# The last layer without the norm, turn and store of rows that no next layer reads; one row store per tile instead of two

## What is computed

```
h = RMSNorm(x) * norm_pre_mix[l]
z = h @ w_in[l]
mixer = concat(retention, mLSTM, gated DeltaNet, NSA)(z) @ w_out[l]
x = x + RMSNorm(mixer) * norm_post_mix[l]
x = x + RMSNorm(ConvFFN(RMSNorm(x) * norm_pre_ffn[l])) * norm_post_ffn[l]
```

## Time and profile before

| what | value |
|---|---|
| median of 3 runs | 4205.48 us |
| profiled execution, its own time | 4212.83 us |
| its span | 4211.0 us |
| TensorE busy | 3765.2 us (89%) |
| VectorE busy | 1950.8 us (46%) |
| ScalarE busy | 1286.9 us (31%) |
| DMA moved | 504.85 MB, mean 120 GB/s |
| mean granted TensorE clock | 0.946 of 2.4 GHz |

### The profile page before, as it was taken

The page is one execution under the profiler, slowest core; times in us unless marked ns, Lnnn a source line. Parts: engine busy times, 40 slices in busy tenths (PEclk is TensorE's granted clock), DMA queues, the critical chain, the costliest instruction groups (busy, mean ns, idle before and its releaser), DMA issues. The chain is left out here.

```text
span 4211.0 us, 55742 instructions
## 1 busy us (share of the span) xinstructions
PE 3765.2 (89%) x22236; PEld 3203.9 (76%) x22236; DVE 1950.8 (46%) x3830; ACT 1286.9 (31%) x2902; POOL 418.9 (10%) x296
## 2 busy tenths in 40 slices
PE   5999698688979999999979987977898899999997
PEld 4888587445658999997768876864475789999875
DVE  3234477663444333335541436776533443333455
ACT  2111255452222221123331114554432322211343
POOL 0035101002201000000000540010021100000000
PEclk9999799798989999999989998997899999999999
DMA  7344322305432222255543433122152422222654
GB/s 246 118 142 161 99 64 61 104 6 204 170 104 89 76 70 66 76 180 206 212 160 105 166 114 97 60 70 79 40 232 105 157 66 76 67 69 84 221 195 179
DMA packets 302046, 504.85 MB, mean 120 GB/s; under 512 B 67381, under 2 KB 226774, under 8 KB 297201
## 3 DMA queue, kind: packets, MB, share of 16 engines
q1 hardware_dynamic: 296523, 426.06, 31.3%
q0 software_dynamic: 4608, 67.11, 3.9%
q10 hardware_dynamic: 656, 8.13, 0.6%
HBM read 386.90 MB, written 129.63 MB: 123 GB/s over the span
## 5 line engine op out<-in xcount | busy, mean ns | idle before, releaser
L1033 PE MATMUL ps<-h_hi,fu_hi 128*128 128x344 f32 x2112 | 682.3, 323 | 10.1 <-DVE h_lo L1255 7.3
L1035 PE MATMUL ps<-h_hi,fu_lo 128*128 128x344 f32 x2112 | 677.6, 321 | 0.0
L1034 PE MATMUL ps<-h_lo,fu_hi 128*128 128x344 f32 x2112 | 677.1, 321 | 0.0
L564 PE MATMUL ps<-zi_whi,h_hi 128*128 128x468 f32 (+1 forms) x1152 | 432.9, 376 | 50.7 <-DVE zi_wlo L645 50.7
L1033 PEld LDWEIGHTS ps<-h_hi,fu_hi 128*128 128x128 f32 x2112 | 398.0, 188 | 14.1 <-DVE h_lo L1255 7.8
L1035 PEld LDWEIGHTS ps<-h_hi,fu_lo 128*128 128x128 f32 x2112 | 398.8, 189 | 0.0
L1034 PEld LDWEIGHTS ps<-h_lo,fu_hi 128*128 128x128 f32 x2112 | 398.2, 189 | 0.0
L568 PE MATMUL ps<-zi_wlo,h_hi 128*128 128x468 f32 (+1 forms) x1024 | 384.2, 375 | 0.0
L569 PE MATMUL ps<-zi_whi,h_lo 128*128 128x468 f32 (+1 forms) x1024 | 384.0, 375 | 0.0
L1059 PE MATMUL ps<-fd_whi,fd_fhi 128*128 128x512 f32 x704 | 278.4, 395 | 15.0 <-DVE fd_flo L1272 14.2
L564 PEld LDWEIGHTS ps<-zi_whi,h_hi 128*128 128x128 f32 x1152 | 217.5, 189 | 80.3 <-DVE h_lo L641 51.9
(11 more groups left out here) (633 smaller groups left out, 6964.2 us busy)
## 6 DMA issues: line engine op xcount, KB each, us to landing
w_ahead<-w_ffn_down SPq DMA_DIRECT2D x44, 1024.0 KB, 5.8
z<-zi_z SPq DMA_DIRECT2D x112, 234.0 KB
zi_h<-z SPq DMA_DIRECT2D x64, 384.0 KB, 4.6
f_all<-fu_f SPq DMA_DIRECT2D x44, 516.0 KB, 3.4
w_ahead<-w_ffn_gate SPq DMA_DIRECT2D x44, 512.0 KB, 4.8
w_ahead<-w_ffn_up SPq DMA_DIRECT2D x44, 512.0 KB, 6.1
fd_raw<-w_ffn_down SPq DMA_DIRECT2D x22, 1024.0 KB, 5.6
zi_raw<-w_in SPq DMA_DIRECT2D x24, 936.0 KB, 5.6
```

Source lines behind the costliest of these rows:

```text
L564: nc.tensor.matmul(out, rows_hi, w_hi[:, i % 2, k, c0], start=(k == 0), stop=False)
L1033: nc.tensor.matmul(out, up_hi[f % 2][:, j, k, :], h_hi[:, k, seg], start=(k == 0), stop=False)
L1034: nc.tensor.matmul(out, up_hi[f % 2][:, j, k, :], h_lo[:, k, seg], start=False, stop=False)
L1035: m = nc.tensor.matmul(out, up_lo[f % 2][:, j, k, :], h_hi[:, k, seg], start=False, stop=(k == KD - 1))
```

## The change

`FINAL` is true in the last layer. There the kernel now leaves out the whole chain from `norm_square` to `norm_store` for all nine tiles, and the load of the next norm's gain. `store(t)` now makes one DMA per tile in both layers: to the output in the last layer, to `x_cur` in the first. The counts that SyncE waits for at the end follow.

```diff
--- before.py
+++ after.py
@@ -712,6 +712,7 @@
     RING = 3
     STEPS = len(GROUPS) * NF
     MOST = max(e - a for a, e in GROUPS)
+    FINAL = l == DEPTH - 1
     STORE_AT = 5
     NORM_AT = {6: 0, 9: 1, 12: 2, 15: 3}
     H_STORE_AT = {7: 0, 8: 1, 9: 2, 10: 3}
@@ -813,6 +814,10 @@
 
             return GROUPS[g - 1][0] + f if g and f < GROUPS[g - 1][1] - GROUPS[g - 1][0] else None
 
+        def normed_tile(g, f, at):
+
+            return earlier(g, at[f]) if f in at and not FINAL else None
+
         def height(t):
             return min(P, TOK - t * P)
 
@@ -923,9 +928,9 @@
 
                 def store(t):
                     sp.wait_ge(S("x2_ready"), t + 1)
-                    sp.dma_start(x_cur[rows(t, height(t)), :], xt[0:height(t), t]).then_inc(S("x_stored"), 16)
+                    kept_row = x_cur[rows(t, height(t)), :]
                     out = io["y_prompt"][0, rows(t), :] if t < NT else io["y_sample"][:, 0, :]
-                    sp.dma_start(out, xt[0:height(t), t]).then_inc(S("x_stored"), 16)
+                    sp.dma_start(out if FINAL else kept_row, xt[0:height(t), t]).then_inc(S("x_stored"), 16)
 
                 other = Loads(sp, S("others"))
                 for pp in range(RING, len(GROUPS) * PAIRS):
@@ -938,21 +943,24 @@
                         sp.wait_ge(S("summed"), 6 * NF)
                         other(gb[:], io["norm_post_ffn"][ds(l, 1), :].rearrange("a n -> (a n)").partition_broadcast(P))
                         other(xt[:], x_cur[0:ROWS, :].rearrange("(t p) n -> p t n", p=P))
-                        norm_gain(kit, io, N, sp, 1 - l)
+                        if not FINAL:
+                            norm_gain(kit, io, N, sp, l + 1)
                     if g and p == STORE_AT:
                         for t in range(*GROUPS[g - 1]):
                             store(t)
-                    if p in H_STORE_AT and earlier(g, H_STORE_AT[p]) is not None:
-                        norm_store(kit, env, N, sp, earlier(g, H_STORE_AT[p]))
+                    if normed_tile(g, p, H_STORE_AT) is not None:
+                        norm_store(kit, env, N, sp, normed_tile(g, p, H_STORE_AT))
                 for t in range(*GROUPS[LAST]):
                     store(t)
-                    norm_store(kit, env, N, sp, t)
+                    if not FINAL:
+                        norm_store(kit, env, N, sp, t)
                 st.all_in()
                 ld.all_in()
                 for r in range(4):
                     sp.wait_ge(S(f"f_stored{r}"), 16 * ((NF - r + 3) // 4))
-                sp.wait_ge(S("x_stored"), 32 * TT)
-                norm_stored(kit, sp)
+                sp.wait_ge(S("x_stored"), 16 * TT)
+                if not FINAL:
+                    norm_stored(kit, sp)
                 other.all_in()
 
             @b.tensor
@@ -1062,9 +1070,9 @@
                         if f == NF - 1 and t + 1 < GROUPS[g_][1]:
                             m.then_inc(S("y_summed"), 1)
                     m.then_inc(S("used"), 1)
-                    if f in NORM_AT and earlier(g_, NORM_AT[f]) is not None:
-                        norm_turn(kit, env, N, pe, earlier(g_, NORM_AT[f]))
-                for t in range(*GROUPS[LAST]):
+                    if normed_tile(g_, f, NORM_AT) is not None:
+                        norm_turn(kit, env, N, pe, normed_tile(g_, f, NORM_AT))
+                for t in range(*GROUPS[LAST]) if not FINAL else ():
                     norm_turn(kit, env, N, pe, t, TAIL_BANK[t])
 
             @b.scalar
@@ -1178,20 +1186,22 @@
                     if s % NF == 0 and s:
                         for t in range(*GROUPS[s // NF - 1]):
                             square(t)
-                    if s % NF + 2 in NORM_AT and earlier(s // NF, NORM_AT[s % NF + 2]) is not None:
-                        norm_square(kit, N, act, earlier(s // NF, NORM_AT[s % NF + 2]))
+                    if normed_tile(s // NF, s % NF + 2, NORM_AT) is not None:
+                        norm_square(kit, N, act, normed_tile(s // NF, s % NF + 2, NORM_AT))
                 t = GROUPS[LAST][0]
                 square(t)
                 square(t + 1)
                 act.wait_ge(S("used"), NF * (LAST + 1))
                 A.activation(low_y[:], ps[LOW:LOW + NB, BANK:BANK + 2, :].rearrange("p a n -> p (a n)"), ACT.Copy).then_inc(S("low_read"), 1)
-                norm_square(kit, N, act, t)
-                norm_square(kit, N, act, t + 1)
+                if not FINAL:
+                    norm_square(kit, N, act, t)
+                    norm_square(kit, N, act, t + 1)
                 square(t + 2)
-                norm_scale_act(kit, N, act, t)
-                norm_scale_act(kit, N, act, t + 1)
-                norm_square(kit, N, act, t + 2)
-                norm_scale_act(kit, N, act, t + 2)
+                if not FINAL:
+                    norm_scale_act(kit, N, act, t)
+                    norm_scale_act(kit, N, act, t + 1)
+                    norm_square(kit, N, act, t + 2)
+                    norm_scale_act(kit, N, act, t + 2)
 
             @b.gpsimd
             def _(pool):
@@ -1202,12 +1212,12 @@
                 for g, (a, e) in enumerate(GROUPS):
                     for t in range(a, e):
                         n = height(t)
-                        if g == LAST and t == SAMPLE:
+                        if g == LAST and t == SAMPLE and not FINAL:
                             norm_root(kit, env, N, pool, t - 2)
                             norm_root(kit, env, N, pool, t - 1)
                         pool.wait_ge(S("y_eps"), t + 1)
                         nc.gpsimd.tensor_tensor(ss[0:n, 2, t:t + 1], ss[0:n, 1, t:t + 1], mhalf[0:n, 0:1], ALU.pow).then_inc(S("y_rms"), 1)
-                    for t in range(a, e) if g < LAST else (TT - 1,):
+                    for t in () if FINAL else range(a, e) if g < LAST else (TT - 1,):
                         norm_root(kit, env, N, pool, t)
 
             @b.vector
@@ -1274,7 +1284,7 @@
 
                 def take(t):
                     wait_sums(dve, t)
-                    if t >= N.depth:
+                    if t >= N.depth and not FINAL:
                         dve.wait_ge(S("x_turned"), t - N.depth + 1)
                     V.tensor_copy(N.row(t)[0:height(t)], sums(t)).then_inc(S("y_taken"), 1)
 
@@ -1287,7 +1297,8 @@
                         dve.wait_ge(S("y_taken"), t + 1)
                     else:
                         wait_sums(dve, t)
-                        dve.wait_ge(S("x_turned"), t - N.depth + 1)
+                        if not FINAL:
+                            dve.wait_ge(S("x_turned"), t - N.depth + 1)
                     dve.wait_ge(S("y_rms"), t + 1)
                     summed = low_y[:] if t == SAMPLE else row if group_of[t] < LAST else sums(t)
                     link(V.scalar_tensor_tensor(row, summed, ss[0:n, 2, t:t + 1], gb[0:n], ALU.mult, ALU.mult))
@@ -1355,24 +1366,26 @@
                     g_, f = s // NF, s % NF
                     if f >= 2 and earlier(g_, f - 2) is not None:
                         residual(earlier(g_, f - 2))
-                    if f + 1 in NORM_AT and earlier(g_, NORM_AT[f + 1]) is not None:
-                        norm_eps(kit, N, dve, earlier(g_, NORM_AT[f + 1]))
-                    if f in NORM_AT and earlier(g_, NORM_AT[f]) is not None:
-                        norm_scale(kit, N, dve, earlier(g_, NORM_AT[f]))
-                    if f - 1 in NORM_AT and earlier(g_, NORM_AT[f - 1]) is not None:
-                        norm_whole(kit, env, N, dve, earlier(g_, NORM_AT[f - 1]))
+                    if normed_tile(g_, f + 1, NORM_AT) is not None:
+                        norm_eps(kit, N, dve, normed_tile(g_, f + 1, NORM_AT))
+                    if normed_tile(g_, f, NORM_AT) is not None:
+                        norm_scale(kit, N, dve, normed_tile(g_, f, NORM_AT))
+                    if normed_tile(g_, f - 1, NORM_AT) is not None:
+                        norm_whole(kit, env, N, dve, normed_tile(g_, f - 1, NORM_AT))
                 t = GROUPS[LAST][0]
                 residual(t)
                 residual(t + 1)
-                norm_eps(kit, N, dve, t)
-                norm_eps(kit, N, dve, t + 1)
+                if not FINAL:
+                    norm_eps(kit, N, dve, t)
+                    norm_eps(kit, N, dve, t + 1)
                 dve.wait_ge(S("low_read"), 1)
                 link(V.tensor_tensor(low_y[:], ps[0:NB, BANK:BANK + 2, :].rearrange("p a n -> p (a n)"), low_y[:], ALU.add), S("sample_whole"))
                 residual(t + 2)
-                norm_whole(kit, env, N, dve, t, TAIL_BANK[t])
-                norm_eps(kit, N, dve, t + 2)
-                norm_whole(kit, env, N, dve, t + 1, TAIL_BANK[t + 1])
-                norm_whole(kit, env, N, dve, t + 2, TAIL_BANK[t + 2])
+                if not FINAL:
+                    norm_whole(kit, env, N, dve, t, TAIL_BANK[t])
+                    norm_eps(kit, N, dve, t + 2)
```

(2 more changed lines are left out.)

## The result

The changed kernel takes 4192.03 us (median of 9 runs, 4190.45 to 4208.24), the kernel before in the same series 4209.35 us (4198.74 to 4220.31). The ratio is 0.9965 with a 95% interval of 0.9954 to 0.9975: 0.35% less, or 14.7 us (10.5 to 19.4) of 4209.35, where 16.4 us were forecast. The interval leaves 1 out, so the changed kernel is faster, by less than 0.5%.

What follows compares the result with a forecast made beforehand. TensorE, busy 3765.2 of 4211.0 us, was taken as the bound, and at stage ends the chain there. Terms 5.2 + 10.0 + 1.2 = 16.4 us off the 4205.48 us median gave 4189.1 us; range 4178 to 4202 us, 8 in 10.

Steps and rivals of the forecast that it cites:

- Six turns: Second layer, tiles 0 to 5, inside the groups: eight transposes each, 0.87 us per turn, 5.2 us saved.
- squares, scalings and gains inside the groups: ScalarE and VectorE work removed in the second layer's groups: worth nothing, since TensorE's full stretches cover it.
- The second layer's tail: From the sample sum to the span's end: earlier sum, norm chain gone, sooner last landing; 10.0 us saved (9.3 to 10.5).
- The sample sum: VectorE in the second layer's tail: can start at 4191.44 in place of 4192.80, 1.36 us earlier.
- The unhindered small store: 32 KB store of the sample rows at the kernel's end: lands in 1.9 us, with 1.4 and 2.6 as ends.
- The first layer's end: Last h store lands in 2.6 us, not 4.0, so the second layer's first load comes earlier: 1.2 us (0 to 1.4).
- Stores inside the groups: Missing 512 KB stores in both layers' groups free DMA engines, but TensorE waits for no load there: 0 us.
- turns not given back: Rival: TensorE finds its inputs late inside the groups, so only 11.2 us are saved, 4194.3 us; chance 0.07.
- turns at full duration: Rival: the six turns cost 48 x 0.272 = 13.1 us, so 24.3 us are saved, 4181.2 us; chance 0.03.
- The granted clock: Rival: second layer's clock level shifts; around 4180 us (chance 0.14), 4200 us (0.07) or 4230 us (0.04).

Runs made afterwards that it cites:

- the doubled turns: Kernel before, with the eight transposes of each turn inside the groups issued twice, in both layers: ratio 1.0033 (1.0022 to 1.0045).
- the stores alone: Kernel before with one store per tile, whole norm chain kept in both layers: profiled once, no ratio; 21.5 us from tile 6's store to the end.
- the norm chain alone: Kernel before without the last layer's norm chain, both row stores kept in both layers: 4198.38 us against 4211.08, ratio 0.9969.
- the first stores put back: Changed kernel with the first layer's output stores put back: profiled once, no ratio; first layer's end 5.83 us, tail 12.75 us.
- the sum first: Changed kernel with the sample rows' sum ahead of tile 7's residual in the last layer's tail: ratio to before 0.9955 (0.9941 to 0.997).

## Why the prediction was right, point by point

- Six turns, forecast 5.2 us from 0.87 each: 5.5 us measured (2.74 + 2.72), 0.91 each, confirmed by putting them back and, at 0.87, by doubling them. That the turns' cost had to be read from starts was right, and that squares, scalings and gains inside the groups are worth next to nothing fits: the doubled turns alone account for 0.87 of the 0.91. What the other 0.04 are was not taken apart.
- The second layer's tail, forecast 10.0 us (9.3 to 10.5): 10.1. The sample sum came forward by the 1.36 us worked out. The unhindered small store took 1.6 us where 1.9 was taken and 1.4 to 2.6 stood as bounds; what follows its landing was 2.0 us where 1.8 was taken. These two errors, -0.3 and +0.2 us, nearly cancel, so part of the closeness of this term is luck.
- The first layer's end, forecast 1.2 us: 1.3, the h store landing after 2.6 us as forecast.
- Stores inside the groups, forecast 0: 0 (the stores alone leave the stretches at 79.02 and 62.85). The prediction counts 8 of 512 KB per layer there; six of them stand inside the groups, two in the tail.
- What the sum lacked: the change of groups in the last layer, 1.6 us more in the pair of profiles. With it the sum is 15.3 us, without it 16.9; the runs say 14.7 (10.5 to 19.4) and can't tell the two apart.
- A slip in the sums: the lower end of the forecast, 5.2 + 9.3 + 0, is 14.5 and not 14.4. Nothing hangs on it.
- The rival of turns not given back falls, since the stretches became shorter by the turns and TensorE had no gap where they stood (69.00 of 69.00 and 58.00 of 58.00 us busy). That of turns at full duration falls by the doubled turns.
- The granted clock was a rival with 0.25 in all. It did come, in the single pair of profiles (11.7 us the wrong way), but it scatters from execution to execution with nothing changed. The medians differ by what the changed parts give (14.7 us, 10.5 to 19.4, against 15.3 or 16.9), which leaves room for a shift of a few us and shows none. Its reason as given, that the second layer starts 1.2 us earlier, was not needed for that: the first layer, with nothing changed ahead of it, scatters as much.
- The base: the sum was taken off the median of the three runs shown, 4205.48 us. The nine of the series have 4209.35, 3.9 us more. So the time of 4192.03 lies 2.9 us above the forecast 4189.1, while the saving as a difference of medians, 17.3 us, lies 0.9 above the forecast 16.4. That the time came so close is luck in part: with both medians scattering by some us, only the distances above tell that the terms were right.

## What to carry to other kernels

In this kernel, where TensorE is busy without a gap, the work of the other engines cost next to nothing (0.04 of the 0.91 us per tile at most), and TensorE's own work cost the distance of starts (0.11 us per transpose) and not durations (0.27 us). Where the stage ends, the links of the chain behind the last matmul count. More than half of the gain (10.1 of 16.9 us) came from there: look for work in the last iteration that only a next iteration would read. And when the change is smaller than the scatter of the executions, compare distances between instructions that both programs have. Here stretches and tails repeat within 0.1 us while the whole scatters by 20. But look for each distance in several profiles, and in a part that wasn't changed: one of them comes in two lengths, 1.6 us apart.

## What was not expected

The change of groups in the last layer takes 17.0 or 18.6 us, with the same waits. Where it takes 18.6 us the granted clock in it is 0.91 (read in all three profiles of the changed kernel and in the second of the kernel before), where it takes 17.0 us it is 1.00: a short phase at the lower of the two levels (1.2 GHz), behind a wait of TensorE of 2.5 us. In all six profiles without the inner turns of the last layer it took 18.6 (18.63, 18.62 and 18.61 in the changed kernel, 18.61, 18.60 and 18.63 in the norm chain alone, the first stores put back and the sum first). With these turns in, it took 17.0 in four of five (17.02, 17.01, 17.05, 17.05) and 18.61 in one; with the turns twice 19.89, at 0.84. That looks like a tie to the length of the full stretch ahead of the wait (76.3, 79.05 and 81.7 us).

The same change of groups in the first layer speaks against that. There the turns stand in every one of these kernels, the stretch ahead is 79.0 us in eleven of the twelve profiles, and the wait is 2.5 to 2.6 us. It took 18.6 us in five of the eleven (among them the first profiles before and after) and 17.0 in six, and 17.03 with the turns twice, behind a stretch of 81.64 us. The first layer of the kernel before, in its first and in its third profile (columns as above):

```profile
2042.89:2061.53 18.64, 16.77 (x65) 11.78 (x65) 14.29 (x22) 6.13 (x10) 1.63 (x4) 0.91 0.42 142
```

```profile
2037.86:2054.88 17.02, 15.15 (x64) 10.69 (x65) 14.28 (x22) 6.13 (x10) 1.62 (x4) 1.00 0.45 155
```

The change of groups before that one, which no kernel here alters, also comes in two lengths: 18.8 to 18.9 us in 18 of 24 places, 17.2 to 17.3 in six. So the same instructions behind a stretch of the same length meet the lower level in one execution and not in the next, and the length of the stretch doesn't decide alone. Six of six without the turns against six of sixteen with them (both layers) may still be more than chance; no kernel here changed that length alone, so it stays open whether the change gives back 1.6 of the 16.9 us that its parts gain, some of it, or nothing.
